# First block's input projection as three fp32r products, weights' low parts on GpSimd

## The reference

```
for l in range(DEPTH):
    hn = rmsnorm(h, norm1_g[l])
    proj = hn @ w_in[l]                       # 1024 -> 2560, float32
    q, k, v, u = split(proj)                  # 512, 512, 512, 1024
    q, k = rope(q), rope(k)
    attn_out = diff_attention(q, k, v, lam, subln_g[l], lam_init)   # 4 heads
    conv_out = conformer_conv(u + b_glu[l], ...)  # a * sigmoid(gate), causal depthwise conv
                                                  # of 31 taps, layer norm over channels, silu
    h = h + concatenate([attn_out, conv_out]) @ w_out[l]
    hn = rmsnorm(h, norm2_g[l])
    gate, up = split(hn @ w_gate_up[l])
    h = h + (silu(gate) * up) @ w_down[l]
```

## Time and profile before

| | |
|---|---|
| median of 3 runs | 2024.46 us (2022.91 to 2025.78) |
| the profiled execution's own time | 2021.76 us |
| its span, first to last instruction | 2019.9 us |
| granted TensorE clock, mean | 0.964 |
| PE busy | 1894.0 us (94%) |
| DVE busy | 849.6 us (42%) |
| ACT busy | 585.1 us (29%) |
| POOL busy | 63.9 us (3%) |

### The profile page before, as it was taken

How to read it: one execution, slowest core, us unless ns; L and a number is a source line. 1 busy time by engine, 2 the same in 40 slices (tenths; PEclk the granted TensorE clock), 3 DMA queues, 4 the chain that set the end, 5 groups by cost and what they waited for, 6 DMA issues and landing times.

```text
span 2019.9 us, 31441 instructions
## 1 busy us (share of the span) xinstructions
PE 1894.0 (94%) x12160; PEld 1484.3 (73%) x12160; DVE 849.6 (42%) x1618; ACT 585.1 (29%) x1051; POOL 63.9 (3%) x55
## 2 busy tenths in 40 slices
PE   7999999899999997998778799999999999999998
PEld 5778999877799996886667798878755555555554
DVE  4956454386654542542556532132522222222222
ACT  2154443312644432123444211010222222222222
POOL 0010000000100000000000340000000000000000
PEclk9999999999999999999889898899899999999999
DMA  6533444454344443333112010223589999999993
GB/s 260 198 139 134 168 182 171 168 209 157 137 146 171 183 184 118 138 137 113 63 63 84 22 60 25 84 98 123 235 342 382 403 394 399 403 391 391 396 400 122
DMA packets 57149, 403.54 MB, mean 200 GB/s; under 512 B 6496, under 2 KB 7904, under 8 KB 8288
## 3 DMA queue, kind: packets, MB, share of 16 engines
q1 hardware_dynamic: 56624, 400.55, 51.3%
q10 hardware_dynamic: 432, 1.71, 0.3%
HBM read 401.19 MB, written 1.05 MB: 199 GB/s over the span
## 4 chain that ended last, share of the span: by engine, by line
PE 88%; DVE 6%; ACT 3%; issue 2%; POOL 0%; DMA 0%; SPq 0%; DVEq 0%; ACTq 0%
PE ps L775 21%; PE ps L1203 18%; PE ps L873 15%; PE ps L578 6%; PE ps L1177 5%; PE ps L1193 3%; PE ps L1120 1%; PE ps L1111 1%; PE ps L535 1%; PE ps L1019 1%; PE ps L1031 1%; PE ps L1032 1%; DVE big L1771 1%; PE ps L943 1%; PE ps L600 1%
## 5 line engine op out<-in xcount | busy, mean ns | idle before, releaser
L873 PE MATMUL ps<-hn,ring 128*128 128x256 f32 x1344 | 315.3, 395 | 3.6 <-ACT hn L1513 3.6
L873 PEld LDWEIGHTS ps<-hn,ring 128*128 128x128 f32 x1344 | 266.4, 200 | 49.2 <-issue 11.5
L775 PE MATMUL ps<-xhi,wlo 128*128 128x272 f32 x800 | 230.4, 288 | 0.0
L775 PE MATMUL ps<-xhi,whi 128*128 128x272 f32 x800 | 229.3, 287 | 0.0
L1834 DVE TENSOR_TENSOR wlo<-ring,whi 128x2048 fp32r<-128x2048 f32 x76 | 174.1, 2291 | 119.0 <-ACT whi L1383 118.9
L775 PE MATMUL ps<-hn_lo,whi 128*128 128x272 f32 x672 | 194.4, 289 | 0.0
L1203 PE MATMUL ps<-big 128*64 128x512 f32 x816 | 181.8, 594 | 0.0
L1203 PE MATMUL ps<-ring,big 128*64 128x512 f32 x816 | 181.7, 594 | 0.0
L1383 ACT ACTIVATE whi<-ring 128x2048 fp32r<-128x2048 f32 x76 | 145.1, 1909 | 83.0 <-PE ps L775 82.7
L578 PE MATMUL ps<-hn,ring 128*128 128x272 f32 x640 | 159.6, 406 | 6.0 <-DVE hn L1743 5.4
L578 PEld LDWEIGHTS ps<-hn,ring 128*128 128x128 f32 x640 | 123.0, 196 | 38.7 <-issue 6.6
(11 more groups left out here) (391 smaller groups left out, 2740.2 us busy)
## 6 DMA issues: line engine op xcount, KB each, us to landing
ring<-in_stream SPq DMA_DIRECT2D x277, 1024.0 KB, 5.0
big<-in_stream SPq DMA_DIRECT2D x102, 1024.0 KB, 9.4
h<-in_xT SPq DMA_DIRECT2D x1, 1088.0 KB, 5.1
big<-in_consts ACTq DMA_DIRECT2D x1, 1088.0 KB, 5.1
out_xT<-h SPq DMA_DIRECT2D x1, 1024.0 KB, 4.7
cst<-in_consts SPq DMA_DIRECT2D x1, 576.0 KB, 6.0
big<-in_consts ACTq DMA_DIRECT2D x1, 326.5 KB, 6.7
big<-in_w_router ACTq DMA_DIRECT2D x1, 256.0 KB, 3.3
```

Of the source, the lines that this page charges most:

```text
L775: m = mm(out, a[:, at_:at_ + P], b[:, k, :], start=first and i == 0, stop=last and i == 2)
L873: m = mm(ps[:, i % 2, n * T:(n + 1) * T], w[:, k, n, :], hm[:, k, :], start=k == 0, stop=k == DC - 1)
```

## The change

The ten w_in slots of a layer are computed as the dense part's are: three fp32r products per call. The rounded copy of a slot is made by ACT into whi0 or whi1 in turn (`high_input`), the low part by POOL in place of the slot. The normalised input is split in four steps of two channel chunks: ACT writes `hin_hi` (over the buffer of squares), DVE writes `hin_lo` in place of hn. The very first chunk takes its products in the order high and low weights by hin_hi first, then high weights by hin_lo. Semaphore counts are shifted by ten slots and four steps. ACT's by-product of `head_out` goes to another buffer, as the old one now lies under hin_hi. The ada slots, the convolution and everything behind are as they were.

```diff
--- before.py
+++ after.py
@@ -96,8 +96,10 @@
 BIG0 = RING * SLOT + 2 * DC * L
 HN0 = BIG0 - DC * L
 DENSE = OUT_SLOTS + GU_SLOTS + DN_SLOTS
+PROJ = [name for name in IN_ORDER if name[:3] != "ada"]
 OVERLAYS = [
     [("yhi", BIG0 + 4096, D), ("ylo", BIG0 + 5120, D), ("STr", BIG0 + 6272, 2, T)],
+    [("hin_hi", BIG0, DC, L)],
     [(f"wlo{j}", j * SLOT, SLOT) for j in range(RING)] + [
         ("xhi", HN0, DC, L), ("hff_lo", BIG0 + 3384, FC, L), ("hff_hi", BIG0 + 9912, FC, L), ("hn_lo", BIG0 + 15896, DC, L),
         ("cat_lo", BIG0 + 18744, DC, L), ("whi2", BIG0 + 22968, SLOT), ("whi0", BIG0 + 25784, SLOT), ("whi1", BIG0 + 27832, SLOT)]]
@@ -197,7 +199,8 @@
         at[0] = attn_end
         wlo = [rounded[f"wlo{j}"] for j in range(RING)]
         whi = [rounded[f"whi{j}"] for j in range(3)]
-        xhi, hn_lo, cat_lo, hff_hi, hff_lo = (rounded[n] for n in ("xhi", "hn_lo", "cat_lo", "hff_hi", "hff_lo"))
+        xhi, hn_lo, cat_lo, hff_hi, hff_lo, hin_hi = (rounded[n] for n in ("xhi", "hn_lo", "cat_lo", "hff_hi", "hff_lo", "hin_hi"))
+        hin_lo = xhi
 
         ps = ctx.enter_context(nc.psum_tensor("ps", [P, 8, 512], F32))
         par2 = sb("par2", [P, NPAR2])
@@ -335,10 +338,10 @@
         attn_out = sem("attn_out", 5)
         gate_act = sem("gate_act", FC)
         hff_ready = sem("hff_ready", FC)
-        whi_ready = sem("whi_ready", DENSE)
-        wlo_ready = sem("wlo_ready", DENSE)
-        xhi_ready = sem("xhi_ready", 5 + DC)
-        xlo_ready = sem("xlo_ready", 5 + DC)
+        whi_ready = sem("whi_ready", IN_SLOTS + DENSE)
+        wlo_ready = sem("wlo_ready", IN_SLOTS + DENSE)
+        xhi_ready = sem("xhi_ready", 9 + DC)
+        xlo_ready = sem("xlo_ready", 9 + DC)
         hff_hi_ready = sem("hff_hi_ready", FC)
         hff_lo_ready = sem("hff_lo_ready", FC)
         chain_v = sem("chain_v")
@@ -567,15 +570,31 @@
                         W(pe, *READER[WORK[i - 4]], l)
                     return ps[:, BANK[name], :]
 
+                def product(out, w, at_, x, k, first, last):
+
+                    hi, lo = x
+                    for i, (a, b) in enumerate(((w[0], hi), (w[1], hi), (w[0], lo))):
+                        m = mm(out, a[:, at_:at_ + P], b[:, k, :], start=first and i == 0, stop=last and i == 2)
+                    return m
+
                 def chunk(slot_name, n, name):
 
-                    s = IN_ORDER.index(slot_name)
-                    w = weights(s)
+                    s, j = IN_ORDER.index(slot_name), PROJ.index(slot_name)
                     bank = take(name)
-                    for k in range(DC):
-                        if s == 0 and n == 0:
-                            W(pe, "hn_ready", k + 1, l)
-                        m = mm(bank[:, 0:L], w[:, k, n, :], hn[:, k, :], start=k == 0, stop=k == DC - 1)
+                    if n == 0:
+                        W(pe, "wlo_ready", j + 1, l)
+                    w = whi[j % 2], wlo[s % RING]
+                    if j == 0 and n == 0:
+                        for k in range(DC):
+                            W(pe, "xhi_ready", k // 2 + 1, l)
+                            for i in range(2):
+                                mm(bank[:, 0:L], w[i][:, 2 * k * P:2 * k * P + P], hin_hi[:, k, :], start=k + i == 0, stop=False)
+                        for k in range(DC):
+                            W(pe, "xlo_ready", k // 2 + 1, l)
+                            m = mm(bank[:, 0:L], w[0][:, 2 * k * P:2 * k * P + P], hin_lo[:, k, :], start=False, stop=k == DC - 1)
+                    else:
+                        for k in range(DC):
+                            m = product(bank[:, 0:L], w, (2 * k + n) * P, (hin_hi, hin_lo), k, k == 0, k == DC - 1)
                     m.then_inc((even_full, slot_done)[n], 1)
 
                 def rotate(name):
@@ -765,15 +784,8 @@
 
                 def both_parts(d, t0=0):
 
-                    W(pe, "wlo_ready", d + 1 + RING * t0, l)
+                    W(pe, "wlo_ready", IN_SLOTS + d + 1 + RING * t0, l)
                     return whi[d % 3], wlo[(OUT0 + d) % RING]
-
-                def product(out, w, at_, x, k, first, last):
-
-                    hi, lo = x
-                    for i, (a, b) in enumerate(((w[0], hi), (w[1], hi), (w[0], lo))):
-                        m = mm(out, a[:, at_:at_ + P], b[:, k, :], start=first and i == 0, stop=last and i == 2)
-                    return m
 
                 def add_out(n, ks, first, last):
                     w = both_parts(n)
@@ -783,7 +795,7 @@
                             W(pe, *READER[[name for name in WORK if BANK[name] == b][-1]], l)
                         for k in ks:
                             if not first and n == 0 and half == 0:
-                                W(pe, "xlo_ready", 2 + k, l)
+                                W(pe, "xlo_ready", 4 + 2 + k, l)
                             m = product(ps[:, b, 0:L], w, (2 * k + half) * P, (xhi, cat_lo), k,
                                         first and k == ks[0], last and k == ks[-1])
                         if last and half == 0:
@@ -792,7 +804,7 @@
                         m.then_inc(slot_done, 1)
 
                 conv_part, attn_part = range(4, 8), range(4)
-                W(pe, "xlo_ready", 1, l)
+                W(pe, "xlo_ready", 4 + 1, l)
                 add_out(0, conv_part, True, False)
                 W(pe, "at_ready", 9, l)
                 for i in range(5):
@@ -820,12 +832,12 @@
                     for n in range(2):
                         for k in range(DC):
                             if n == 0:
-                                W(pe, "xhi_ready", 5 + k + 1, l)
+                                W(pe, "xhi_ready", 9 + k + 1, l)
                             for i in range(2):
                                 c = (2 * k + n) * P
                                 mm(ps[:, n, 0:L], w[i][:, c:c + P], xhi[:, k, :], start=k + i == 0, stop=False)
                     for k in range(DC):
-                        W(pe, "xlo_ready", 5 + k + 1, l)
+                        W(pe, "xlo_ready", 9 + k + 1, l)
                         for n in range(2):
                             c = (2 * k + n) * P
                             m = mm(ps[:, n, 0:L], w[0][:, c:c + P], hn_lo[:, k, :], start=False, stop=k == DC - 1)
@@ -1311,11 +1323,24 @@
                 def work(name, n):
                     return ps[:, BANK[name], 0:n]
 
+                def high_input(j):
+
+                    s = IN_ORDER.index(PROJ[j])
+                    act.wait_ge(ring_full[s % RING], (l * (LAYER_SLOTS // RING) + s // RING + 1) * 16)
+                    if j >= 2:
+                        slot_out(IN_ORDER.index(PROJ[j - 2]))
+                    f(whi[j % 2][:, :], ring[:, s % RING, :], ACT.Copy).then_inc(whi_ready, 1)
+
                 squares(l, 0, lambda g: 1)
+                high_input(0)
                 root_of_mean(l, 0, small[:, 60:61])
+                high_input(1)
                 W(act, "lam_step", 2, l)
                 f(small[:, 2:4], ps[:, 6, 0:2], ACT.Exp).then_inc(lam_step, 1)
                 W(act, "par_ready", 1, l)
+                for c in range(0, DC, 2):
+                    W(act, "hn_ready", c + 2, l)
+                    f(hin_hi[:, c:c + 2, :], hn[:, c:c + 2, :], ACT.Copy).then_inc(xhi_ready, 1)
 
                 def gate_out(c):
                     chunk_out(f"glu{c}", 1)
@@ -1372,7 +1397,7 @@
                 def head_out(u):
                     W(act, "o_full", u + 1, l)
                     f(o_tail if u == 6 else o_sb[:, u - (u > 6), :], ps[:, 7, 0:P], ACT.Copy)
-                    f(sq[:, 0, 0:P], ps[:, 7, 0:P], ACT.Square, accum_out=small[:, 40 + u:41 + u]).then_inc(o_squared, 1)
+                    f(sgl[:, 0, 0:P], ps[:, 7, 0:P], ACT.Square, accum_out=small[:, 40 + u:41 + u]).then_inc(o_squared, 1)
 
                 def high_weights(d, t0=0):
 
@@ -1380,21 +1405,27 @@
                     act.wait_ge(ring_full[s % RING], (l * (LAYER_SLOTS // RING) + t0 + s // RING + 1) * 16)
                     if d >= 3:
                         act.wait_ge(slot_done, l * LAYER_SLOTS + RING * t0 + s - 2)
+                    elif d < 2:
+                        slot_out(IN_ORDER.index(PROJ[8 + d]))
                     f(whi[d % 3][:, :], ring[:, s % RING, :], ACT.Copy).then_inc(whi_ready, 1)
 
                 for c in range(3):
+                    high_input(c + 2)
                     gate_out(c)
                     if c == 2:
                         columns_out(0)
                     rows_out(c)
+                high_input(5)
                 gate_out(3)
                 rows_out(3)
                 raw_out("q0")
                 columns_out(1)
                 raw_out("k0")
+                high_input(6)
                 rows_out(4)
                 value_out(0)
                 value_out(1)
+                high_input(7)
                 turned_value_out(0)
                 exps(0)
                 rows_out(5)
@@ -1403,12 +1434,14 @@
                 exps(1)
```

(20 more changed lines are left out.)

## The result

The change makes the kernel slower. The changed kernel's median is 2085.65 us (2084.84 to 2086.59, four runs), against 2024.95 for the kernel before on the same chip: a ratio of 1.0312, 95% interval 1.0297 to 1.0328. The forecast was 2080 with a range of 2035 to 2106. The profiled execution took 2085.85 us.

What follows compares the result with a forecast made beforehand. VectorE was taken as the bound from first gate to column sums, PE after. To 2021.76 us it added starts +8.4 and +4.6, POOL +57.2, matmuls -7.9, waits -4.0, together +58.3: 2080, range 2035 to 2106.

Steps and rivals of the forecast that it cites:

- The likeliest case: Whole kernel: POOL subtractions hold up VectorE's taps for their full length, total 2080 us; chance 0.55.
- The lock: In the tap run, seven POOL subtractions a layer block VectorE instructions with two SBUF inputs: 28.6 us a layer, +57.2.
- j=1: POOL's subtraction asked for as the hn operations begin: half of 4.5 us at each start, +4.6 together.
- The starts: Before the first gate, ScalarE's copies and hn's low parts delay it by 3.8 us and 4.6 us, +8.4 together.
- Matmuls behind the tap: After the last convolution tap, five half slots (k2, q3, k3, V2, V3) save 3.95 us a layer: -7.9.
- j=9 falls where DVE has slack: Behind the last tap, POOL's last subtraction of a layer was given no cost, as VectorE has slack.
- DVE's waits for q1 and k1: In the tap run, faster matmuls bring q1 and k1 earlier, removing VectorE's waits: 2.0 us a layer, -4.0.
- The end: From the reciprocal of the convolution's layer norm to that of the next norm: no term in the sum.
- Cold PE: PE runs at half clock after long waits; with lost overlap up to 10 us of uncertainty, outside the sum.
- side by side: Rival: POOL and VectorE hinder each other only in the seen direction or hardly, 2018 or 2010 us; chance 0.15.
- Sharing in pieces: Rival: POOL gives way within its instruction, so a tap waits for part: 2051 us, 2035 to 2060; chance 0.17.
- The worse case: Rival: unbroken taps keep POOL out, low parts come late, PE waits and runs cold: 2100 to 2120; chance 0.13.

Runs made afterwards that it cites:

- e9: The changed kernel with the first 90 of 124 taps a layer reading a constant PSUM bank as second input, convolution sum left out there: 2069.36 us, ratio 1.0231.
- e4: The changed kernel with GpSimd's subtraction j=1 waiting for the low parts of hn and j=9 for the third softmax difference: 2081.57 us, ratio 1.0275.
- e8: e1 with GpSimd subtracting whole slots for j=1 and j=9, 8 columns for the other eight; low parts of weights left out: 2044.42 us, ratio 1.0100.
- e1: The changed kernel with GpSimd's subtractions cut to 8 columns and the high part read for the low one: 2031.85 us, ratio 1.0045.
- e7: The kernel before with only the last two slots, qk3 and v23, as three fp32r products, low parts on VectorE: 2023.73 us, ratio 1.0001.
- e10: e1 with each of the first four gates ahead of ScalarE's copy in its queue; low parts of weights left out: 2017.55 us, ratio 0.9980.
- e5: The changed kernel with each GpSimd subtraction cut into four instructions of 512 columns: 2080.15 us, ratio 1.0275.
- e11: The whole changed kernel with each of the first four gates ahead of ScalarE's copy in its queue: 2090.31 us, ratio 1.0325.

## Why the prediction was right

The sum was +58.3 us, the profiled executions differ by 2085.85 - 2021.76 = 64.1. The likeliest case came out, with its mechanism. Term by term:

- **The lock** (the 28.6 us a layer, less 2.0 of DVE's waits: +53.2 for both). Measured +48.1. Between gate and column sums the taps are 12.5 us busier than before (64.6 against the 52.1 of the earlier trace rows), the first taps' tensor_scalar 9.4, and two tensor_tensor of one element per partition, L1859, 4.1 (two at the usual 0.16 would be 0.3):

```profile
L1807 DVE SCALAR_TENSOR_TENSOR big<-big,par 128x272 f32<-128x272 f32 x120 | 64.6, 598 | 0.9
L1805 DVE TENSOR_SCALAR big<-big,par 128x272 f32<-128x272 f32 x4 | 11.1, 2780 | 0.1
L1859 DVE TENSOR_TENSOR small<-small 128x1 f32<-128x1 f32 x2 | 4.4, 2202 | 0.1
```

  Together 26.0 us for seven subtractions, 3.7 each where 4.1 were forecast. The direction unseen before and the places were right, the number nearly. More lay under gates than the 0.2 us that the forecast allowed, since POOL, held back by a tap run, enters just when a gate with PSUM input is due. The Trainium skill, SBUF — State Buffer, section "Who interferes with whom", says that the two exclude each other whichever starts first; the trace agrees in both directions (a tap of 4821 ns behind POOL, a POOL subtraction of 7265 ns behind taps), and e9's PSUM inputs bear out its condition. Who wins where both want to go on is another matter: at 58.80 four taps that began after POOL's instruction went first.
- **j=1** (half of 4.5 us, twice: +4.6). It got in just ahead of the hn operations in both layers, 7.63 against 3.39 us, and makes +8.1 of the starts' +14.8. Half was assumed where the whole came true. e4 takes 4.1 away from each start, and e8 brings 4.3 and 4.0 back.
- **The starts** (+8.4 without j=1). Measured by e1, +1.8 and +4.9, 6.7 together: layer 1 as forecast (4.6), layer 0 2.0 below it. The two differ by the kernel before, not by e1, whose starts are 15.46 and 15.50 with a clock of 0.89 in both: before, layer 0 ran at 0.75 and layer 1 at 1.00, worth 3.1 us (e7). The forecast gave this 0.8 us (3.8 against 4.6). e10 shows that the part behind the copy was 3.3 a start.
- **Matmuls behind the tap** (-7.9). This is the step that failed: "j=9 falls where DVE has slack". Measured -1.0. Without the lock the tails give back 3.1 and 2.0 (e1). With it, L1852 stands still for 4.0 us at 139.07, beside the POOL subtraction of 138.48, and it feeds the exponentials of a head. VectorE was 45% busy there, but a chain between engines passes through it, so slack in busy time was no slack in time. The tails of the change are 2.0 longer than e1's, those of e8 3.0. And of the 3.95 a layer, no more than the 2.0 to 3.1 of e1 would have come.
- **DVE's waits for q1 and k1** (-4.0). They are gone in the change: in its tap runs VectorE waits 0.0 us for ACT before the first rotations (L1826), where before it was 2.1, and all its idle time fell from 3.9 to 1.9 us a layer. But the reason was luck. The forecast had PE bring q1 and k1 earlier; yet in e1, where PE is as fast and the lock is away, the rotations still wait 1.9 us, and they stop only when the gates stand ahead of ACT's copies (0.4 in e10). In the change it is VectorE that comes later, held by POOL.
- **The end** was forecast unchanged and is 2.3 longer. It takes about 53.5, 54.7, 55.6 or 55.9 us in the various runs. Part of it is the clock: 0.97 over the end before (53.5), 0.94 in the change (54.7). The two ends of e7, which are the same code, show what that is worth: PE is busy for 48.0 us at 0.97 and for 49.3 at 0.94. It is not all of it, for e1's end has 0.94 too and takes 55.6. The rest is open, and so is why the clock falls there.
- **Cold PE**, TensorE at the lower clock after a wait, was rightly foreseen. After its waits the granted clock is 0.50 (1.2 of 2.4 GHz), as at the column sums both before and after the earlier trace rows. In the tap run it cost little, for PE waits for VectorE there anyway; in starts and ends it is worth the 3.1 and 1.3 us of e7.

```profile
51.80:55.40 3.60, 3.60 (x16) 3.60 (x17) 3.60 (x10) 0.00 (x0) 0.00 (x0) 0.50 0.00 0
128.20:132.20 4.00, 3.97 (x9) 3.04 (x10) 1.21 (x3) 0.00 (x0) 0.00 (x0) 0.50 0.00 0
```

Of the rivals, side by side is refuted by e1, e8 and e9 together, and its 2018 is what e10 reaches (2017.55) only with no low parts of weights and the gates first. Sharing in pieces is refuted by taps of 4.8 us. The worse case, POOL kept out by unbroken taps, exists (6.43 and 7.26 us), but the tap run as a whole stayed below the forecast; no run separates what the worse case cost. That the sum came within 6 us owes something to compensation: measured less forecast, the lock is -5.1 and the starts -1.7, j=1 +3.5, the tails +6.9 and the ends +2.3, +5.9 in all, and the stretches measured make 64.2 where the forecast had 58.3.

## What to carry to other kernels

Before work is moved from VectorE to an idle GpSimd, list what VectorE runs beside it and where its inputs lie. Beside a run of operations on SBUF tensors the price is most of the length of the GpSimd instruction, on VectorE's path: here 3.7 of its 4.5 us on the "free" engine, against 2.29 on the full one. Look also for short VectorE operations between engines in stretches where it seems slack, since a lock of 4 us shows there in full; and when an ACT copy is added to a queue, see whether it stands ahead of what feeds the critical engine. Before a few us are put down to an edit, compare the granted clock of the stretch in both traces: here two passes through the same code differ by 3.1 us with it.

## What the runs showed that was not expected

- The smallest operations are held as long as the largest: tensor_tensor on 128x1 for 2.5 us and more, tensor_scalar on 128x2 for 4.0 (usual 0.17). A tensor_scalar with one SBUF tensor and parameters from SBUF waits as well (4.12 us), while a scalar_tensor_tensor with one input in PSUM never did (at most 499 ns of 180).
- A POOL that only writes delays that tensor_scalar by up to 1.3 us (1709 against some 420 ns), and the taps by at most 0.36 (848 against 491).
- Who gets in is not settled by how closely the taps follow each other. Two runs of 21 taps, 0.41 us apart, kept POOL out until they ended (58.80 and 71.20), and a run of eight at the same distance let it in after its fourth (100.10). Once a tap had been stopped in e5, the two engines took turns, instruction by instruction. What decides was not tested.
- The same exchange in ACT's queue gave 13 to 14 us without whole subtractions on POOL (e10) and nothing with them (e11).
- The same code takes one of two or three lengths, by TensorE's granted clock: the start 10.6 or 13.6 us, the end 53.5 or 54.8, and the untouched rest behind layer 1 1455 or 1457.5 us.
